# Fold products between the down jobs, folds one place earlier, Fourier results ahead of the normed chunks, and the third gate tile split in the attention part

## The reference, cut to what matters

```python
# layers 0 and 1 (first_block)
sh1, sc1, ga1, sh2, sc2, ga2 = jnp.split(silu(c) @ w_mod[l] + b_mod[l], 6)   # also for c_ctx
h = modulate(rmsnorm(x, g_norm1[l]), sh1, sc1)
pf, mq, mk, mv, mo, mg, cq, ckv, kr = split_proj(h @ w_in[l])
y_f = fourier_mix(pf)                       # real part of a 2D FFT over tokens and group columns
y_m = mLSTM(...); y_a = latent attention(...)
x = x + ga1 * (concatenate([y_f, y_m, y_a]) @ w_out[l])
x = x + ga2 * (square(relu(modulate(rmsnorm(x), sh2, sc2) @ w_up[l])) @ w_down[l])
# layers 2 and 3 (second_block)
h = rms(x) * (1 + sc1) + sh1;  parts = split(h @ w_in[l])
y_a = gqa_attention(...) @ w_branch_a[l];  y_b = dilated_attention(...) @ w_branch_b[l]
x = x + gt1 * ((sigmoid(parts[-2]) * y_a + sigmoid(parts[-1]) * y_b) @ w_out[l])
x = x + gt2 * (square(relu(h2 @ w_ff1[l])) @ w_ff2[l])
```

## Time and profile before

| what | value |
|---|---|
| three runs | 3656.46, 3662.9 and 3669.1 us, median 3662.9 us |
| the profiled execution | 3666.42 us |
| its span | 3664.6 us |
| PE busy | 3491.9 us, 95% |
| DVE busy | 2131.2 us, 58% |
| ACT busy | 1225.1 us, 33% |
| POOL busy | 310.6 us, 8% |
| mean granted clock of TensorE | 0.978 |

### The profile page before, as it was taken

How to read it: one execution, slowest core, us unless ns; L and a number is a source line. 1 busy time by engine, 2 the same in 40 slices (tenths; PEclk the granted TensorE clock), 3 DMA queues, 4 the chain that set the end, 5 groups by cost and what they waited for, 6 DMA issues and landing times.

```text
span 3664.6 us, 45096 instructions
## 1 busy us (share of the span) xinstructions
PE 3491.9 (95%) x17152; PEld 2742.0 (75%) x17152; DVE 2131.2 (58%) x2847; ACT 1225.1 (33%) x1516; POOL 310.6 (8%) x320
## 2 busy tenths in 40 slices
PE   7998999999998898899997999999999999999999
PEld 3676868888887676678885577778887567778887
DVE  6456557646667465576666565267667665355343
ACT  1235444122113245342223333333223443333222
POOL 0000102001001000010000010001011000001000
PEclk9999999999999998999998999999999999999999
DMA  8221202322332121034441011225443111222222
GB/s 335 76 76 52 73 2 91 127 92 92 117 112 77 53 79 70 24 129 168 163 163 62 31 66 57 81 104 186 165 165 115 49 53 58 73 100 93 102 92 103
DMA packets 52252, 359.58 MB, mean 98 GB/s; under 512 B 5960, under 2 KB 6600, under 8 KB 11024
## 3 DMA queue, kind: packets, MB, share of 16 engines
q1 hardware_dynamic: 35744, 256.92, 19.9%
q10 hardware_dynamic: 16368, 100.73, 7.5%
HBM read 355.31 MB, written 2.32 MB: 98 GB/s over the span
## 4 chain that ended last, share of the span: by engine, by line
PE 52%; issue 32%; DVE 10%; ACT 4%; DMA 1%; POOL 1%; DVEq 0%; ACTq 0%; POOLq 0%
PE pair L540 21%; PE pair L1036 10%; PE pair L607 3%; PE pair L1106 2%; PE pair L552 1%; PE pair L578 1%; DVE arena L2196 1%; PE pair L653 1%; PE pair L710 1%; DVE w_lo L2111 1%; PE pair L869 1%; PE pair L958 1%; ACT w_hi L1396 1%; PE pair L1181 1%; PE pair L933 1%
## 5 line engine op out<-in xcount | busy, mean ns | idle before, releaser
L2111 DVE TENSOR_TENSOR w_lo<-raw,w_hi 128x2048 fp32r<-128x2048 f32 x221 | 506.4, 2291 | 266.2 <-ACT w_hi L1396 259.7
L1396 ACT ACTIVATE w_hi<-raw 128x2048 fp32r<-128x2048 f32 x221 | 421.5, 1907 | 642.7 <-PE pair L540 589.7
L540 PE MATMUL pair<-h_hi,w_hi 128*128 128x512 f32 (+2 forms) x1856 | 601.6, 366 | 5.7 <-DVEq L2093 2.7
L540 PE MATMUL pair<-h_hi,w_lo 128*128 128x512 f32 (+2 forms) x1856 | 598.8, 365 | 0.0
L540 PE MATMUL pair<-h_lo,w_hi 128*128 128x512 f32 (+2 forms) x1856 | 598.1, 364 | 0.0
L540 PE MATMUL pair<-u_hi,w_hi 128*128 128x512 f32 (+3 forms) x1152 | 387.0, 372 | 24.5 <-DVE x L2152 13.1
L540 PE MATMUL pair<-u_hi,w_lo 128*128 128x512 f32 (+3 forms) x1152 | 384.4, 370 | 0.0
L540 PE MATMUL pair<-u_lo,w_hi 128*128 128x512 f32 (+3 forms) x1152 | 384.3, 370 | 0.0
L2196 DVE SCALAR_TENSOR_TENSOR arena<-arena,cact 128x256 f32<-128x256 f32 x756 | 369.7, 512 | 19.5
L2347 DVE TENSOR_TENSOR u_lo<-arena,u_hi 128x512 fp32r<-128x512 f32 (+1 forms) x128 | 97.1, 759 | 459.9 <-POOL arena L2875 455.0
L540 PEld LDWEIGHTS pair<-h_hi,w_hi 128*128 128x128 f32 (+2 forms) x1856 | 311.9, 184 | 68.7 <-issue 7.3
(11 more groups left out here) (352 smaller groups left out, 4919.9 us busy)
## 6 DMA issues: line engine op xcount, KB each, us to landing
raw<-in_wt_dram SPq DMA_DIRECT2D x222, 1024.0 KB, 4.8
arena<-in_modw_dram ACTq DMA_DIRECT2D x78, 1024.0 KB, 5.0
arena<-in_modw_dram SPq DMA_DIRECT2D x18, 1024.0 KB, 7.5
arena<-negm_rows_dram ACTq DMA_DIRECT2D x16, 384.0 KB, 4.0
arena<-in_fconst_dram ACTq DMA_DIRECT2D x2, 2688.0 KB, 10.1
x<-in_xt_dram SPq DMA_DIRECT2D x1, 3072.0 KB, 16.5
arena<-in_brope_dram ACTq DMA_DIRECT2D x4, 640.0 KB, 3.9
out_dram<-x SPq DMA_DIRECT2D x1, 2048.0 KB, 7.2
```

Of the source, the lines that this page charges most:

```text
L540: mm = pe.matmul(pp[p][0:m, lo:hi], a[0:rows, k * width + c0:k * width + c0 + m], b[0:rows, k, lo:hi], start=(k == 0 and i == 0), stop=(k ...
L1396: act.activation(w_hi[slot][:], raw[slot][:], ACT.Copy).then_inc(w_hi_done, 1)
L2111: dve.tensor_tensor(w_lo[slot][:], raw[slot][:], w_hi[slot][:].bitcast(F32), ALU.subtract)\
```

## The change

It has three parts.

1. In the MLPs, PE's products of the three folded tiles no longer stand in one run. The first tile's follow down job c = 0 of the second down tile, the second's follow c = 1, and the third's stand at the end of the group (in the last group both the second's and the third's follow c = 1). On DVE the first fold of the first group moves from behind the fourth `u_lo` to ahead of it. In the last group each fold moves forward by one `u_lo`, and with them the step that adds up the next layer's modulation (`next_half_mod`).
2. In layer 1 (`n > S`), ACT and DVE call `first_features` ahead of chunk 3, not 5, and DVE makes the four copies to `f_v` right behind it, ahead of chunks 3 to 7.
3. In the dilated attention's second pass, ACT splits the third gate tile ahead of `high(0)` and `sums()`, and DVE ahead of `low(0)` and `scaled(1)`. `gates` does one split less on both engines.

```diff
@@ -718,8 +718,8 @@
                     part(c, (3,)).then_inc(job_dve, 1)
 
             def mlp_group(n, layer, i, first_group, last=False):
-                def folds():
-                    for s in range(MOD_RING):
+                def folds(part):
+                    for s in part if layer < 3 else ():
 
                         pe.wait_ge(mod_folded, t.next(mod_folded) + MOD_RING)
                         folded_products(MOD_RING, i, s, fold_ring[s], 2 if layer == 0 else 1).then_inc(mod_used, 1)
@@ -745,10 +745,10 @@
                     for c in range(2 if half == 0 else 0, 4):
                         feature_job(w, 4, P, c * P, P, 512, U, n, (4 * half + c + 1) % 3,
                                     tile_used if c == 3 else job_dve)
-                        if last and layer < 3 and half and c == 0:
-                            folds()
-                if layer < 3 and not last:
-                    folds()
+                        if half and c < 2:
+                            folds((1, 2) if last and c else (c,))
+                if not last:
+                    folds((2,))
 
             def mlp(n, layer):
                 mlp_group(n, layer, 0, True)
@@ -1395,10 +1395,10 @@
                 act.wait_ge(tile_used, t.next("split"))
                 act.activation(w_hi[slot][:], raw[slot][:], ACT.Copy).then_inc(w_hi_done, 1)
 
-            def job(last=False):
+            def job(last=False, ahead=0):
                 if last:
 
-                    act.wait_ge(tile_used, t.now("split", 1))
+                    act.wait_ge(tile_used, t.now("split", 1 - ahead))
                 else:
                     act.wait_ge(job_act, t.next(job_act))
 
@@ -1491,7 +1491,7 @@
                 if early:
                     early()
                 for j in range(KC):
-                    if first and j == 5:
+                    if first and j == (3 if n > S else 5):
                         first()
 
                     act.wait_ge(dve_act, t.next(dve_act))
@@ -2009,6 +2009,7 @@
                         split()
                         probs(1, 2, 1)
                         probs(1, 3, 0)
+                        split()
                         high(0)
                         sums()
 
@@ -2019,10 +2020,10 @@
                 for c in range(2):
                     act.activation(gate[0][:, c, :], gate[0][:, c, :], ACT.Sigmoid)
                 for i in range(1, 8):
-                    if i > 1:
+                    if i > 2:
                         split()
                     for c in range(2):
-                        job(last=c == 1)
+                        job(last=c == 1, ahead=1 if i == 1 else 0)
                         b = c if i == 1 else (2 * i + c + 2) % 4
                         finish(act.activation(gate[i // 4][:, 2 * (i % 4) + c, :], bank(b), ACT.Sigmoid), pair_free[b],
                                *([gates_in] if i == 7 and c else []))
@@ -2275,6 +2276,12 @@
                 for c in range(2):
                     job(last=c == 1)
                     dve.tensor_tensor(f_pf[:, c, 0:S], pp[c][:, 0:S], late_r[:, 0:S], ALU.mult).then_inc(first_out, 1)
+                values_read(NT)
+
+            def values_read(nt):
+                for i in range(nt):
+                    job()
+                    dve.tensor_copy(f_v[:, i, :], pp[i % 2][:, 0:512]).then_inc(pair_free[i % 2], 1)
 
             def first_rope():
                 shift_sum(2)
@@ -2340,18 +2347,16 @@
                         else:
                             split()
                         for c in range(2):
-                            if half and c == 0 and not first and not last:
+                            if half and c == (1 if first else 0) and not last:
                                 ring_fold(0)
                             dve.wait_ge(hid_hi, t.next(hid_hi))
                             dve.wait_ge(hid_full, t.next(hid_full) + 2)
                             dve.tensor_tensor(u_lo[:, 2 * half + c, 0:n], m_f[c][:, 0:n], U32[:, 2 * half + c, 0:n],
                                               ALU.subtract).then_inc(hid_lo, 1)
-                            if last and layer < 3 and 2 * half + c:
-                                if half == 0:
+                            if last and layer < 3 and 2 * half + c < 3:
+                                if 2 * half + c == 0:
                                     next_half_mod()
-                                ring_fold(2 * half + c - 1)
-                    if first:
-                        ring_fold(0)
+                                ring_fold(2 * half + c)
                     for half in range(2):
                         split()
                         for c in range(4):
@@ -2377,9 +2382,8 @@
                     dve.wait_ge(rows_turned, 5)
                     dve.wait_ge(fold_used, MOD_FOLD)
                     set_half(1, PG2)
-                for i in range(n // P):
-                    job()
-                    dve.tensor_copy(f_v[:, i, :], pp[i % 2][:, 0:512]).then_inc(pair_free[i % 2], 1)
+                if n > S:
+                    values_read(NTC)
                 for c in range(2):
                     heard()
                     dve.tensor_tensor(u_lo[:, c, 0:n], pp[c][:, 0:n], U32[:, c, 0:n], ALU.subtract)\
@@ -2778,12 +2782,13 @@
                         split()
                         by_key(2, 1)
                         by_key(3, 0)
+                        split()
                         low(0)
                         scaled(1)
                 low(1)
 
             def gates():
-                for i in range(6):
+                for i in range(5):
                     split()
 
                 dve.wait_ge(gates_in, t.next(gates_in))
```

## The result

| | before | changed |
|---|---|---|
| median of four runs of each | 3664.77 us | 3623.68 us |
| lowest to highest | 3656.46 to 3669.1 | 3622.43 to 3625.52 |
| ratio, 95% interval | | 0.9891, [0.9872, 0.9910] |
| the profiled execution | 3666.42 us | 3623.0 us |

The changed kernel is 1.1% faster. The forecast was 3617, its range 3600 to 3643. Measured once more, beside the last experiment, the changed kernel took 3619.3 (3615.7 to 3628.4) at a ratio of 0.9875 [0.9859, 0.9892].

A forecast was written before the change was run, and what follows sets the result against it. PE, busy for 95% of the span, was taken as the bound, so only its pauses and pace count. Terms of 12.6, 13.8, 11.5, 11.7 and 1.0 less 1.6 made 49.0 off 3666.4: 3617 us, range 3600 to 3643.

The forecast's parts named there:

- Layer 0's loop: Layer 0's MLP loop: cutting each run of 24 products into three removes five clock falls of 2.8 us; 12.6 kept.
- The rival that the product runs are not the cause: Layer 0's loop: product runs do not cause the falls, or short ones act as one long; 36.4 gained, 3630; chance 0.13.
- Layers 1 and 2: MLP loops of layers 1 and 2: nothing counted for the product runs' new places, 0 us.
- The gate tiles: Third gate tile, layers 2 and 3: earlier split removes 8.0 us of pauses and 5.8 of slow clock, 13.8.
- The Fourier part: Layer 1's Fourier part: pauses shrink by 6.6 us and the clock gives 4.9, together 11.5.
- Last groups: Last MLP groups of layers 0, 1, 2: second pause goes, net 6.6 us, plus 5.1 of clock, 11.7.
- First groups: First MLP groups of three layers: a pause moves into first_down rather than going; 1.0 us gained, between -4 and +5.
- The 1.6 taken off for new falls: Deduction from the sum of 50.6: the clock may fall behind layer 0's longer pause and the moved ones, 1.6 us.

The follow-up runs named there:

- e3: Kernel before with only VectorE's folds in the first and last groups moved, each group's products left in one run: 3658.9 us, ratio 0.9981.
- e7: Changed kernel with layer 0's 24 products of a group in one run at its end again: 3629.0 us, ratio 0.9907.
- e2: Kernel before with only the third gate tile's split moved: 3651.1 us, ratio 0.9961.
- e1: Kernel before with only the Fourier part of the change (earlier call in layer 1, value copies right behind it): 3652.4 us, ratio 0.9962.
- e4: Kernel before with only the products of each group spread over three places, no fold moved: 3663.8 us, ratio 0.9990.
- e6: Changed kernel with the last group's third fold later, first groups' fold 0 halved around the fourth u_lo, layers 1 and 2 products in one run: 3615.4 us.
- e9: The changed kernel measured and profiled once more, with no edit: 3619.3 us, ratio 0.9875.
- e5: Changed kernel with the last group's third fold moved behind residual c = 1 of the first down tile: 3621.3 us, ratio 0.9876.

## Why the prediction was right, and where a step failed

**The sum.** 49.0 were forecast, 43.4 came in the profiled pair and 41.1 on the medians. The sign, the mechanism of three of the five terms and their sizes held.

**Layer 0's loop is the term that was mis-sized: 12.6 forecast, 6.4 in the two profiles, and 4 to 5 when more executions are counted.** Two readings failed. First, the prediction took a fall (3.41 at half pace) and "a slightly wider spacing of the matmuls for the rest of the group" for one effect, since in its trace they came together. They are two. Four kinds of group show it: 69.25 (no fall, narrow), 70.52 (no fall, wide; e3), 70.82 (fall, narrow; e7) and 72.02 (fall, wide). (Two groups have a fall twice as long: 73.61, wide, in e2 and 72.39, narrow, in e3.) So a fall costs 1.5 to 1.6 and the wide spacing 1.2 to 1.3. That a fall costs less than the 1.7 of the prediction, half of its 3.41 us, can be read from PE's rows of the kernel before, in a group of narrow spacing, in a fall, and in a group of wide spacing:

```profile
719.21 0.51 PE L540 MATMUL pair<-u_lo,w_hi 128*128 128x512 f32 x2
719.55 0.51 PE L540 MATMUL pair<-u_hi,w_lo 128*128 128x512 f32 x2
...
732.55 0.84 PE L540 MATMUL pair<-h_lo,w_hi 128*128 128x512 f32 x2
733.19 0.84 PE L540 MATMUL pair<-h_hi,w_lo 128*128 128x512 f32 x2
...
791.05 0.51 PE L540 MATMUL pair<-u_lo,w_hi 128*128 128x512 f32 x2
791.40 0.52 PE L540 MATMUL pair<-u_hi,w_lo 128*128 128x512 f32 x2
```

A row is a pair, one matmul of 512 columns and one of 256. At 0.50 pairs start 0.64 apart; at 1.00 they start 0.347 apart (narrow) or 0.353 (wide, both as means over a group), which is more than half of 0.64. So 3.41 us at 0.50 do the work of 1.85 to 1.88, and cost 1.53 to 1.56. The three-way cut removes the falls and leaves the spacing wide in every group, also in the first one, which had been narrow. That gives five falls of 1.5 to 1.6 less 1.3 for the first group, 6.2 to 6.7; measured 6.4. Second, the prediction took five falls in five inner intervals for the rule. Over the five kernels with runs of 24 (before, e1, e2, e3, e7), 23 of 35 runs have a fall beginning behind them or in their last microseconds. (The eighth run of 24, in the last group of four of them, has one behind it in e1 alone.) The loop of the profiled execution before, 429.4, was a slow one: with e1 (423.9), e2 (429.4), e3 (425.3) and e7 (427.0) the mean is 427.0. The loop is 423.0 in all seven kernels with shorter runs, 4.0 less. Counted from POOL's squares like this, the loop leaves out what lies behind the first product run; from PE's first job behind that run to the first square of the last group it is 438.5, as the mean, against 433.7. So the part is worth 4.8 in layer 0 on average, and less the 1.4 of the other layers 3.4. The 3.7 of e4 contains this in its interval, but nothing as well.

That the runs bring the clock down was right, if not each time. None of the runs of 8 or 16, in seven kernels with seven groups each, has a fall behind it, 0 of 49 groups against 23 of 35. The rival that the product runs are not the cause is refuted, though its time, 3630, lay as near as the forecast's 3617. The Trainium skill ("TensorE: Matmul & The Clock Gate", section "What's actually happening") lets the clock fall after idleness. PE had no pause in any of these intervals and the clock fell in 23 of them, so here the measurement decides. The same section says that the monitor runs freely and that one kernel changes its clock at different places in different runs; the two profiles of the changed kernel, 6.4 apart in one stage by the falls in it, agree.

**Layers 1 and 2.** I counted nothing for the interruptions. Each group pays 0.12 (45.04 for 44.92), 1.4 over twelve loop groups, and e6 gave it back with one run.

**The gate tiles.** 13.8 forecast, 12.8 measured, 14.3 for the part alone. At the tiles themselves it is 14.0 in the changed kernel; one new fall in layer 3 took 1.2 of it back. That 14.0 is so near to 13.8 is in part luck: no wait at all is left, where I had 0.3 for each, and the clock gave 5.4 where I had 5.8. The u_hi of ACT's list did slip by 0.84 behind the moved split (from 10.28 to 11.12 after the last 1024-column score), as worked out, and PE did not feel it.

**The Fourier part.** 11.5 and 11.5. The pause of 1.58, the four jobs in one row, 0.83 and the unchanged 1.6 ahead of the output products are all as the prediction had them.

**Last groups.** 11.7 and 12.0. The second pause is gone in all three. The one inside `first_down` is 3.33 in layer 0 (3.8 forecast) and unchanged at 1.67 in the others. All three folds of layer 0 met POOL's square: the 14 instructions of the last one took 7.60, against 6.38 without.

```profile
1118.24 7.60 DVE L2197 SCALAR_TENSOR_TENSOR arena<-arena,cact 128x256 f32<-128x256 f32 x14
...
1126.06 0.96 DVE L2354 TENSOR_TENSOR u_lo<-arena,u_hi 128x768 fp32r<-128x768 f32 x1 [0.22 <-DVE arena L2197]
```

The row shows 1.2 for a meeting, less than the 1.5 of a whole POOL instruction that the Trainium skill's rule ("SBUF — State Buffer", section "Who interferes with whom") would give by the prediction's estimate.

**First groups.** 1.0 forecast, -1.4 measured, within the bounds given. The pauses did change places: 2.34 in `first_down` against 2.1 forecast in layer 0, and 2.28 for 2.20 in layers 1 and 2. But behind the one in layer 2 the clock now fell (2461.56, above), which it had not done behind the old one; that is 1.8 of this term. In layer 1 it fell behind both. More traces bear this out: behind the moved pause of layer 2 the clock fell in all six kernels that have it, and behind the old one in none of four. In layer 0, where it did not fall in this profile, it fell in three of six. The 1.6 taken off for new falls were meant for this.

**The falls elsewhere.** The other stages gave 3.5 that nothing in the change explains. Two profiles of the changed kernel itself (the first and e9) differ by 2.3 in the stage between layers 0 and 1 and by 6.4 in the next one. The four parts alone show the same: a stage that an edit did not touch moves by several microseconds between executions with the places of the falls. A profile pair cannot size a term to better than this, only a stage in which neither trace has a fall.

## What to carry to other kernels

When a trace shows two things together in a few places (here a fall of the clock and a wider spacing), do not price them as one, and do not make a rule of five out of five from a single execution: four more traces showed both separately and the rule as two in three. A long run of tiny matmuls can cost more than its own time although the profile shows PE busy throughout. Cutting it into pieces between real jobs was cheap here; where the runs were short already, the cut only cost. Before filling a pause, ask which engine ends last at the next barrier: of the three pauses that e5 removed, one came back there and one in small waits.

## What the runs showed of the hardware

- The granted clock fell to 0.50 behind or in runs of 24 one-column products, 2.73 us long, with PE busy before, in and behind them: 23 of 35 in the loops. Behind 15 runs of 16 (1.84 us) and the runs of 8 (0.95 us) of layer 0's MLP it never did.
- A stretch of 3.41 us at 0.50 cost 1.50 to 1.57 us of a group, not 1.7: pairs start 0.64 us apart in it, and 0.347 or 0.353 at 1.00.
- The same pause had a fall behind it in some executions and none in others: 2.34 us in layer 0's first group, three of six. The 3.3 to 3.5 us of layer 0's last group had one in all five kernels that have it, and the 1.7 us of layers 1 and 2 in none.
- At a granted clock of 1.00 the same pairs of a 512- and a 256-column matmul run in two steady spacings: 69.25 or 70.52 for a group of 410 records, and 0.1733 or 0.1767 for a matmul between the product runs. Behind the 35 long runs it was the narrow one 14 times. Within layer 0's loop the spacing changed only at the long product runs, with a fall or without, and stayed for a whole group; with short runs it was the wide one in all loop groups of seven kernels. What sets it is open; up to 1.3 in each of seven groups of layer 0 hang on it.
- Two more interruptions of a down tile by four short products cost 0.12 us in layers 1 and 2, where a 512-column pass is alone; in layer 0 two or three runs in a group made no difference (70.52 in both).
